# The attention output product of layer 2 as one level of Strassen in 14 block pieces

## The chip, the cores and the metric

The kernel runs on one core of a Trainium2 chip. The metric is the device time of one execution in microseconds. In the profile PE is TensorE's matmul, PEld its weight load, DVE is VectorE, ACT ScalarE, POOL GpSimd and SP SyncE.

## What is computed

Two layers on x of 512 tokens by 1024 features, all in float32. Layer 1 is a differential attention and a retention; layer 2 is a gated convolution and a sliding-window attention. The change is in layer 2:

```python
y_c = b_c * causal_depthwise_conv(c_c * v_c, conv_w)
y_c = y_c * jax.nn.silu(z_c)
y_a = jnp.einsum('bsc,cd->bsd', y_c, w_conv_out)
...
o = sliding_window_attention(q, k, v, sinks) * jax.nn.silu(z_a)
y_b = jnp.einsum('bsc,cd->bsd', o, w_attn_out)
gates = jax.nn.sigmoid(gate_logits + gate_b)
g_a, g_b = jnp.split(gates, N_BRANCHES, axis=-1)
merged = g_a * y_a + g_b * y_b
return x + jnp.einsum('bsd,de->bse', merged, w_out)
```

The product in question is `o` (512 by 1024) with `w_attn_out` (1024 by 1024).

## The kernel before

Everything runs through one stream of **weight pieces**, numbered n, of 128 by 1024 float32 (512 KB). SP loads piece n into slot n mod 4 of a ring (`w_raw`, which shares its memory with `w_lo`), once piece n - 4 is done (`wait_room`). GpSimd rounds it to `w_hi` (`round_piece`, L723), VectorE makes the rest, `w_lo = w_raw - w_hi` (`split_piece`, L1142), and TensorE multiplies. A product of two split operands is three matmuls: hi by hi, lo by hi, hi by lo (L1736 to L1738, in `products`). GpSimd and VectorE prepare piece n + 3 in their program's step n (`ROUNDED_AT`, `SPLIT_AHEAD = 3`).

Each engine's program is written out by hand as a loop over n in two halves; it waits on counting semaphores. Four pieces form a unit. Of layer 2, units 14 to 21 (pieces 56 to 87) are the convolution's inputs; beside them runs the windowed attention, step by step, up to piece 80, and its value (`gT2`) is split into `o2_hi` and `o2_lo` in the steps "OS" on VectorE (L1679, L1680). Units 22 and 23 (**pieces 88 to 95**, `U_AOUT`) are the attention output product, 24 matmuls of 512 columns each; ScalarE copies the banks to `y_b` (L968). Units 24 and 25 (96 to 103, `U_COUT`) are the convolution's output product in the same form, into `part`. From piece 104 (`GATES`) the two gate products and then (`FINAL`) the last product follow, both as one level of Strassen: seven block products A11, A12, S2, S1, S4, S3, A22 of 256 tokens, combined on VectorE.

The Strassen products need four sums of blocks of the weights. They are made in DRAM (`w_sums`): SP **copies** a block of 512 by 512 (1 MB, `copy_block`), and GpSimd's queue adds others to it by an **accumulating DMA** (`gather`, L751, 1 MB; its third and fourth step of a group wait for the landing of the ones before). Before, there are three groups of four: the two gates' and the last product's. The copies stand at pieces 20 to 27 and 48 to 51, the gathers at pieces 56, 59, 62 and so on, every third, up to 89. SP waits for the gathers of a group before it loads the first piece from it.

PSUM has eight banks: four of `proj`, two of `score`, `bank_t` and `bank_o`.

Of the kernel before, what the change touches and what calls it, by code (L numbers as in the profile page):

```python
# [30 lines left out]
P = 128  # L31
# [37 lines left out]
GROUPS = 3  # L69
# [18 lines left out]
COPY_AT = [*range(4 * U_GA, 4 * U_O0), *range(4 * U_Z0, 4 * U_Z1)]  # L88
SUM_AT = [4 * U_Z1 + 4 + 3 * i for i in range(4 * GROUPS)]
# [7 lines left out]
def slot_of(n):  # L97

    if n < GATES:
        return n % SLOTS  # L100
    return RING + n - GATES if n < GATES + EARLY else (n - GATES - EARLY) % RING
# [15 lines left out]
def unit_columns(u):  # L117
# [28 lines left out]
X_AGAIN_AT = range(4 * U_O0 + 3, 4 * U_O0 + 7)  # L146
XS_HOOKS = (7, 7, 8, 9)
# [127 lines left out]
def build(nc, a):  # L275
    with ExitStack() as ctx:
# [121 lines left out]
        m_hi = sb("m_hi", [P, KC, S], F32R, stack=later)  # L398
        logit = sb("logit", [P, 2, 2, 2, 256], stack=later)
# [35 lines left out]
        v_sum = spare[:, 0:2, 256:512]  # L435

# [10 lines left out]

        def pair_of(t, c, r):
# [35 lines left out]
        def wait_room(eng, n):  # L484
# [7 lines left out]
            elif n >= GATES:  # L492
                eng.wait_ge(piece_done, 4 * U_COUT)
# [95 lines left out]
        def wait_tile(eng, u, j):  # L589
# [3 lines left out]
            else:  # L593
                eng.wait_ge(piece_done, 4 * u + j + 1)
# [20 lines left out]

        N_PARAMS = 18
# [4 lines left out]
        def _(sp):  # L621
            def load_piece(n):
                u, q = divmod(n, 4)
                raw, landed = ring(n)[0], raw_landed[slot_of(n)]
                if n >= GATES:
# [51 lines left out]
            for n in range(SLOTS, PIECES):  # L677
# [1406 lines left out]
```

## Time and profile before

| | us |
|---|---|
| median of 3 runs | 816.91 (816.64 to 817.4) |
| the profiled execution | 816.7 |
| its span, first to last instruction | 814.7 |
| PE busy | 808.5 |
| VectorE, ScalarE, GpSimd busy | 609.4, 321.9, 182.6 |

The span lies inside the execution's time; about 2 us stand around it. In the tables below, times are microseconds from the start of the span; the attended product takes 604.6 to 648.1, the convolution's output product follows up to 691.6, then the gates up to 772.3.

### The profile page before, as it was taken

The page shows a single profiled execution, that of the slowest core. Times are in us where ns is not written, and L with a number is a line of the kernel's source. Part 1 is how long each engine was busy: PE and PEld are TensorE (multiplying, and loading weights), DVE is VectorE, ACT ScalarE, POOL GpSimd, SP SyncE. Part 2 cuts the span into 40 slices and gives each one's busy share as a digit, 9 for nine tenths or more (in the row PEclk, how much of TensorE's full clock was granted, in tenths as well). Part 3 has the DMA queues.
Part 4 walks back from the last instruction along what each step waited for, and adds up shares of the span by engine and source line. Part 5 has one row for each costly group of instructions (what it writes and reads, how often), then busy time and mean ns, then how long its engine had stood idle before and what let it go on. Part 6 is the DMA issues. An engine that isn't in the chain of part 4 may idle for free.

```text
span 814.7 us, 11429 instructions
## 1 busy us (share of the span) xinstructions
PE 808.5 (99%) x4220; PEld 687.1 (84%) x4220; DVE 609.4 (75%) x1096; ACT 321.9 (40%) x701; POOL 182.6 (22%) x189
## 2 busy tenths in 40 slices
PE   9999999999999999999999999999999999999998
PEld 7778888888888888888888888888888888999986
DVE  4998778768984476885579788978952269599998
ACT  4374465632212255334445554441000122355580
POOL 2212111111111221121324445444323224000000
PEclk9999999999999999999999999999999999999999
DMA  7332214445143222653365555566876335866562
GB/s 239 87 97 77 79 52 153 158 157 179 53 155 126 82 83 77 208 175 90 91 130 130 125 119 120 128 130 155 168 165 158 104 88 145 233 182 183 182 205 78
DMA packets 129565, 108.92 MB, mean 134 GB/s; under 512 B 4525, under 2 KB 101350, under 8 KB 129510
## 3 DMA queue, kind: packets, MB, share of 16 engines
q1 hardware_dynamic: 123142, 95.60, 38.4%
q0 software_dynamic: 6336, 12.58, 9.4%
q8 instruction: 34, 0.56, 0.3%
q14 instruction: 21, 0.17, 0.1%
q10 hardware_dynamic: 32, 0.01, 0.0%
HBM read 106.08 MB, written 27.26 MB: 164 GB/s over the span
## 4 chain that ended last, share of the span: by engine, by line
PE 92%; DVE 5%; issue 1%; ACT 1%; DVEq 0%; ACTq 0%
PE proj L1736 24%; PE proj L1738 24%; PE proj L1737 24%; PE bank_t L1750 3%; PE bank_o L1825 2%; DVE x L1447 1%; DVE w_lo L1142 1%; PE score L1738 1%; PE score L1737 1%; PE score L1736 1%; PE score L1900 1%; PE score L1899 1%; PE score L1811 1%; PE score L1810 1%; PE bank_o L1918 1%
## 5 line engine op out<-in xcount | busy, mean ns | idle before, releaser
L723 POOL TENSOR_SCALAR w_hi<-w_raw 128x1024 fp32r<-128x1024 f32 x109 | 128.8, 1182 | 436.2 <-DMA w_raw<-in_w_in_dram 310.8
L1142 DVE TENSOR_TENSOR w_lo<-w_raw,w_hi 128x1024 fp32r<-128x1024 f32 x145 | 179.9, 1244 | 60.2 <-POOL w_hi L723 59.6
L1736 PE MATMUL proj<-xt_hi,w_hi 128*128 128x512 f32 (+1 forms) x448 | 171.1, 382 | 0.0
L1738 PE MATMUL proj<-xt_hi,w_lo 128*128 128x512 f32 (+1 forms) x448 | 168.1, 375 | 0.0
L1737 PE MATMUL proj<-xt_lo,w_hi 128*128 128x512 f32 (+1 forms) x448 | 167.8, 375 | 0.0
L1738 PEld LDWEIGHTS proj<-xt_hi,w_lo 128*128 128x128 f32 x448 | 84.4, 188 | 15.5
L1737 PEld LDWEIGHTS proj<-xt_lo,w_hi 128*128 128x128 f32 x448 | 84.5, 189 | 14.2
L1736 PEld LDWEIGHTS proj<-xt_hi,w_hi 128*128 128x128 f32 x448 | 84.5, 189 | 13.9
L1736 PE MATMUL proj<-w_hi,xt_hi 128*128 128x512 f32 x152 | 61.0, 401 | 0.2 <-ACT prob L922 0.2
L1738 PE MATMUL proj<-w_hi,xt_lo 128*128 128x512 f32 x152 | 59.5, 392 | 0.0
L1737 PE MATMUL proj<-w_lo,xt_hi 128*128 128x512 f32 x152 | 59.4, 391 | 0.0
L835 ACT ACTIVATE w_hi<-w_raw 128x1024 fp32r<-128x1024 f32 x36 | 36.9, 1049 | 9.6 <-DMA w_raw<-w_sums 3.8
L1736 PE MATMUL proj<-w_hi,yc_hi 128*128 128x512 f32 x96 | 38.9, 406 | 0.0
L1738 PE MATMUL proj<-w_hi,yc_lo 128*128 128x512 f32 x96 | 37.6, 392 | 0.0
L1737 PE MATMUL proj<-w_lo,yc_hi 128*128 128x512 f32 x96 | 37.4, 390 | 0.0
L1736 PEld LDWEIGHTS proj<-w_hi,xt_hi 128*128 128x128 f32 x152 | 28.6, 188 | 6.9 <-ACT prob L922 0.7
L1038 ACT ACTIVATE prob<-prob,neg_mx 128x512 f32<-128x512 f32 x32 | 22.9, 716 | 28.3 <-DVE neg_mx L1546 28.3
L1080 ACT ACTIVATE prob<-prob,neg_m 128x128 f32<-128x128 f32 x64 | 25.0, 391 | 22.3 <-DVE sink_m L1652 22.3
L1738 PEld LDWEIGHTS proj<-w_hi,xt_lo 128*128 128x128 f32 x152 | 28.5, 188 | 6.2
L1737 PEld LDWEIGHTS proj<-w_lo,xt_hi 128*128 128x128 f32 x152 | 28.6, 188 | 6.0 <-issue 0.2
L734 POOL TENSOR_SCALAR_AFFINE_SELECT yc_hi<-pT 128x512 fp32r<-128x512 f32 x28 | 17.6, 646 | 71.4 <-ACT pT L1094 71.4
L1543 DVE CUSTOM_DVE_ANT_0 prob<-score,table 128x512 f32<-128x512 f32 x32 | 20.8, 688 | 16.1 <-PE score L1811 16.1
(420 smaller groups left out, 1774.4 us busy)
## 6 DMA issues: line engine op xcount, KB each, us to landing
w_raw<-in_w_in_dram SPq DMA_DIRECT2D x79, 512.0 KB, 3.8
w_sums<-in_w_in_dram SPq DMA_DIRECT2D x8, 1024.0 KB, 7.5
w_raw<-w_sums SPq DMA_DIRECT2D x32, 256.0 KB, 3.3
w_raw<-in_w_out_dram SPq DMA_DIRECT2D x14, 512.0 KB, 3.3
w_raw<-in_w_in_dram SPq DMA_DIRECT2D x26, 256.0 KB, 3.6
w_sums<-w_sums POOLq DMA_DIRECT2D x6, 1024.0 KB, 9.9
w_sums<-in_w_out_dram SPq DMA_DIRECT2D x4, 1024.0 KB, 6.8
w_sums<-in_w_in_dram POOLq DMA_DIRECT2D x4, 1024.0 KB, 9.9
```

Source lines behind the costliest of these rows:

```text
L723: pool.tensor_scalar(hi, raw, 1.0, 1.0, ALU.mult, ALU.mult).then_inc(hi_done, 1)
L734: pool.affine_select(out=pT_hi[:, c, :, :], in_=pT[:, 0, :, :], compare_op=op, fill=0.0, base=base, pattern=pattern, channel_multiplier=step)
L835: act.activation(hi, raw, ACT.Copy).then_inc(block_hi_done, 1)
L1038: act.activation(prob[:, m % 2, mp, :], prob[:, m % 2, mp, :], ACT.Exp, bias=neg_mx[:, m % 2, mp:mp + 1], accum_out=den[:, m % 2, mp:mp + ...
L1080: act.activation(prob2[:, m % 2, r, 0:P], prob2[:, m % 2, r, 0:P], ACT.Exp, bias=neg_m2[:, m % 4, r:r + 1], accum_out=den2[:, m % 4, r:r + 1])
L1142: dve.tensor_tensor(lo, raw, hi.bitcast(F32), ALU.subtract).then_inc(w_split, 1)
L1543: dve.tensor_tensor_reduce(prob[:, sl, mp, :], score[:, mp, :], table[:, h % 2, CENTRE - i * P:CENTRE - i * P + S], 1.0, -3e38, ALU.subtra ...
L1736: pe.matmul(out, left[0], right[0], start=first, stop=False)
L1737: pe.matmul(out, left[0], right[1], start=False, stop=False)
L1738: return pe.matmul(out, left[1], right[0], start=False, stop=last)
L1750: last = pe.transpose(dst, src, ident[:])
L1825: last = pe.matmul(bank_o[:, i * P:(i + 1) * P], wT[:, m % 2, c * P:(c + 1) * P], va[:, c, h * P:(h + 1) * P], start=(c == 0), stop=(c == 3))
```

## The change

The attended product becomes one level of Strassen. Pieces 88 to 101 (`AOUT` to `COUT`) are now 14 block pieces: for each pair of column tiles the seven products in the order A11, A12, A22, S2, S1, S4, S3, each with 2 x 4 x 3 matmuls of 256 columns. Its weights come in rows of 256 columns, from `w_attn_out_2` or from a fourth group of sums. The convolution's output product is at 102 to 109, the gates start at 110.

- GpSimd makes the four sums of blocks of the attended values in place in `gT2`, by two-input operations of 128 by 4 x 256, in its steps 84, 85, 85 and 86.
- ScalarE rounds them (steps 87 and 88), VectorE makes their low parts (steps 88, 88, 89, 90).
- In "OS" the rounding to `o2_hi` goes from VectorE to ScalarE; of the first four tiles only 256 tokens are split.
- VectorE combines the products (`combine_out`): seven operations of 512 columns for each seven products. The factor 0.5 of the copy to `y_b` moves into the gating (0.25 instead of 0.5).
- The sums of weights have 16 copies, all at pieces 12 to 27, and 16 gathers, the new group first, at pieces 53, 55, 57, 59, 62 and so on, the last five at 77, 80, 82, 84 and 86.
- The second piece of the convolution's output product waits for the last combination.

```diff
+OUT_PIECES = 7 * 2
+OUT_ORDER = [A11, A12, A22, S2, S1, S4, S3]
-COPY_AT = [*range(4 * U_GA, 4 * U_O0), *range(4 * U_Z0, 4 * U_Z1)]
-SUM_AT = [4 * U_Z1 + 4 + 3 * i for i in range(4 * GROUPS)]
+COPY_AT = range(4 * U_RQK, 4 * U_O0)
+GROUP_ORDER = [ATTENDED, 0, 1, 2]
+SUM_AT = [4 * U_Z1 + 1 + 9 * i // 4 for i in range(4 * GROUPS)]
...
+SO_SUM_AT = (AOUT - 4, AOUT - 3, AOUT - 3, AOUT - 2)
+SO_HI_AT = ((AOUT - 1, 0), (AOUT - 1, 1), (AOUT, 0), (AOUT, 1))
+SO_LOW_AT = ((AOUT, 0), (AOUT, 1), (AOUT + 1, 1), (AOUT + 2, 1))
...
+            def attended_sum(i):
+
+                x11, x12, x21, x22 = (quarter(gT2, row, col) for row in range(2) for col in range(2))
+                if i == 0:
+                    pool.wait_ge(o2_split, KC)
+                    pool.tensor_tensor(x22, x22, x21, ALU.subtract).then_inc(so_summed, 1)
+                elif i == 1:
+                    pool.wait_ge(so_summed, 1)
+                    pool.tensor_tensor(x21, x11, x21, ALU.subtract).then_inc(so_summed, 1)
...
+                if product == A12:
+                    dve.tensor_tensor(out(0, 0), u_sum, psum, ALU.add).then_inc(out_combined, 1)
+                elif product == S2:
+                    dve.tensor_tensor(w_sum, u_sum, psum, ALU.subtract).then_inc(out_combined, 1)
...
+                elif product == S3:
+                    dve.scalar_tensor_tensor(out=out(1, 1), in0=v_sum_out, scalar=-1.0, in1=psum, op0=ALU.mult, op1=ALU.subtract).then_inc(out_combined, 1)
+                    dve.tensor_tensor(w_sum, w_sum, psum, ALU.add).then_inc(out_combined, 1)
+                    dve.wait_ge(out_combined, 7 * pair + 6)
+                    dve.tensor_tensor(out(1, 0), w_sum, kept, ALU.add).then_inc(out_combined, 1)
...
+                for j in range(2):
+                    for k in range(4):
+                        last = products(out_bank(x)[:, j, :], [t[:, k, j * P:(j + 1) * P] for t in w], [t[:, k, :] for t in left], k == 0, k == 3)
+                last.then_inc(piece_done, 1)
```

GpSimd's queue around the start of the attended product. Before, from the rounding of piece 85 to that of 92 (`raw_landed3` is the landing in slot 3, and so on; the DMA rows are gathers):

```order
L723 TENSOR_SCALAR w_hi<-w_raw 128x1024 [waits piece_done,raw_landed1]
L723 TENSOR_SCALAR w_hi<-w_raw 128x1024 [waits piece_done,raw_landed2]
L751 DMA w_sums<-in_w_out_2_dram 512x512
L723 TENSOR_SCALAR w_hi<-w_raw 128x1024 [waits piece_done,raw_landed3]
L723 TENSOR_SCALAR w_hi<-w_raw 128x1024 [waits piece_done,raw_landed0]
L723 TENSOR_SCALAR w_hi<-w_raw 128x1024 [waits piece_done,raw_landed1]
L751 DMA w_sums<-w_sums 512x512 [waits w_gathered2]
L723 TENSOR_SCALAR w_hi<-w_raw 128x1024 [waits piece_done,raw_landed2]
L723 TENSOR_SCALAR w_hi<-w_raw 128x1024 [waits piece_done,raw_landed3]
L723 TENSOR_SCALAR w_hi<-w_raw 128x1024 [waits piece_done,raw_landed0]
```

And after, from the rounding of piece 85 to that of 90:

```order
L775 TENSOR_SCALAR w_hi<-w_raw 128x1024 [waits piece_done,raw_landed1]
L803 DMA w_sums<-in_w_out_2_dram 512x512
L775 TENSOR_SCALAR w_hi<-w_raw 128x1024 [waits piece_done,raw_landed2]
L775 TENSOR_SCALAR w_hi<-w_raw 128x1024 [waits piece_done,raw_landed3]
L810 TENSOR_TENSOR gT2<-gT2 128x4x256 [waits o2_split]
L803 DMA w_sums<-w_sums 512x512 [waits w_gathered2]
L775 TENSOR_SCALAR w_hi<-w_raw 128x1024 [waits piece_done,raw_landed0]
L813 TENSOR_TENSOR gT2<-gT2 128x4x256 [waits so_summed]
L816 TENSOR_TENSOR gT2<-gT2 128x4x256 [waits so_summed]
L775 TENSOR_SCALAR w_hi<-w_raw 128x1024 [waits piece_done,raw_landed1]
L819 TENSOR_TENSOR gT2<-gT2 128x4x256 [waits so_summed]
L803 DMA w_sums<-w_sums 512x512 [waits w_gathered2]
```

The four sums and two more gathers now stand ahead of the rounding of piece 90, and one step of the gathers' chain follows the other after two pieces instead of three.

VectorE at the same place, after, from the split of piece 90 (before, ten splits in a row stand there):

```order
L1232 TENSOR_TENSOR w_lo<-w_raw,w_hi 128x1024 [waits hi_done]
L1405 TENSOR_TENSOR so_lo<-gT2,so_hi 128x1024 [waits so_hi_done,so_summed]
L1232 TENSOR_TENSOR w_lo<-w_raw,w_hi 128x1024 [waits hi_done]
L1405 TENSOR_TENSOR so_lo<-gT2,so_hi 128x1024 [waits so_hi_done,so_summed]
L1232 TENSOR_TENSOR w_lo<-w_raw,w_hi 128x1024 [waits hi_done]
L1425 TENSOR_TENSOR y_b<-th2,proj 128x2x256 [waits out_first,piece_done]
L1405 TENSOR_TENSOR so_lo<-gT2,so_hi 128x1024 [waits so_hi_done,so_summed]
L1232 TENSOR_TENSOR w_lo<-w_raw,w_hi 128x1024 [waits hi_done]
L1405 TENSOR_TENSOR o2_lo<-gT2,o2_hi 128x4x256 [waits so_hi_done,so_summed]
L1232 TENSOR_TENSOR w_lo<-w_raw,w_hi 128x1024 [waits hi_done]
L1427 TENSOR_TENSOR acc<-th2,proj 128x512 [waits out_combined,piece_done]
```

The low parts of the sums and the combinations stand between the splits, each combination behind the split of the piece three further on. At the end of the product the last one, for piece 101, stands behind the split of piece 104:

```order
L1232 TENSOR_TENSOR w_lo<-w_raw,w_hi 128x1024 [waits hi_done]
L1434 SCALAR_TENSOR_TENSOR y_b<-gT2,score 128x2x256 [waits out_combined,piece_done]
L1435 TENSOR_TENSOR acc<-acc,score 128x512
L1437 TENSOR_TENSOR y_b<-acc,proj 128x2x256 [waits out_combined]
L1232 TENSOR_TENSOR w_lo<-w_raw,w_hi 128x1024 [waits hi_done]
```

Behind them on TensorE the second convolution piece waits for the last of these three.

## Rows read from the trace of the kernel before

**Rows 1.** The page: PE's busy time, and granted clock in 40 slices.

```profile
PE 808.5 (99%) x4220; PEld 687.1 (84%) x4220; DVE 609.4 (75%) x1096; ACT 321.9 (40%) x701; POOL 182.6 (22%) x189
...
PEclk9999999999999999999999999999999999999999
```

**Rows 2.** Timeline of PE (start us, us, line, op, tiles): first matmuls of stages and pieces.

```profile
604.61 0.39 PE L1736 MATMUL proj<-o_hi,w_hi 128*128 128x512 f32 x1
...
648.13 0.39 PE L1736 MATMUL proj<-yc_hi,w_hi 128*128 128x512 f32 x1
...
720.44 0.28 PE L1736 MATMUL bank_t<-sx_hi,w_hi 128*128 128x256 f32 x1
...
723.32 0.28 PE L1736 MATMUL bank_o<-sx_hi,w_hi 128*128 128x256 f32 x1
```

**Rows 3.** Busy time of each engine while the attended product runs.

```profile
core 0: us, PE busy (x) PEld busy (x) DVE busy (x) ACT busy (x) POOL busy (x), PEclk, DMA share, GB/s
604.60:648.10 43.50, 43.50 (x193) 36.04 (x192) 12.38 (x13) 4.80 (x8) 10.69 (x9) 1.00 0.58 139
```

**Rows 4.** Timeline of GpSimd: roundings of pieces 85 to 91 and two gathers.

```profile
580.20 1.05 POOL L723 TENSOR_SCALAR w_hi<-w_raw 128x1024 fp32r<-128x1024 f32 x1 [8.11 <-DMA w_raw<-in_w_in_dram]
...
583.44 1.03 POOL L751 DMA_DIRECT2D w_sums<-in_w_out_dram  x1
586.83 1.04 POOL L723 TENSOR_SCALAR w_hi<-w_raw 128x1024 fp32r<-128x1024 f32 x1 [2.36 <-DMA w_raw<-in_w_in_dram]
595.67 1.24 POOL L723 TENSOR_SCALAR w_hi<-w_raw 128x1024 fp32r<-128x1024 f32 x1 [7.79 <-DMA w_raw<-in_w_attn_out_dram]
597.65 1.97 POOL L723 TENSOR_SCALAR w_hi<-w_raw 128x1024 fp32r<-128x1024 f32 x1 [0.74 <-DMA w_raw<-in_w_attn_out_dram]
599.57 1.03 POOL L751 DMA_DIRECT2D w_sums<-w_sums  x1
...
612.88 1.05 POOL L723 TENSOR_SCALAR w_hi<-w_raw 128x1024 fp32r<-128x1024 f32 x1 [8.55 <-DMA w_raw<-in_w_attn_out_dram]
```

**Rows 5.** Timeline of VectorE: a cast slowed, a cast alone, convolution passes, splits.

```profile
582.50 1.28 DVE L1679 CAST o_hi<-gT 128x512 fp32r<-128x512 f32 x1
...
584.42 0.42 DVE L1679 CAST o_hi<-gT 128x512 fp32r<-128x512 f32 x1
...
595.25 2.20 DVE L1293 SCALAR_TENSOR_TENSOR acc<-cv,cols,acc 128x512 f32<-128x512 f32 x2
597.48 1.22 DVE L1142 TENSOR_TENSOR w_lo<-w_raw,w_hi 128x1024 fp32r<-128x1024 f32 x1
```

**Rows 6.** DMA issues (KB, us to landing) at 568.99, 572.16, 583.04, 588.48, 599.36, 599.57, 604.80.

```profile
w_sums<-in_w_out_dram POOLq DMA_DIRECT2D x1, 1024.0 KB, 9.8
...
w_raw<-in_w_in_dram SPq DMA_DIRECT2D x1, 512.0 KB, 8.0
...
w_raw<-in_w_in_dram SPq DMA_DIRECT2D x1, 512.0 KB, 3.7
...
w_raw<-in_w_attn_out_dram SPq DMA_DIRECT2D x1, 512.0 KB, 7.1
...
w_raw<-in_w_attn_out_dram SPq DMA_DIRECT2D x1, 512.0 KB, 3.8
...
w_sums<-w_sums POOLq DMA_DIRECT2D x1, 1024.0 KB, 11.9
...
w_raw<-in_w_attn_out_dram SPq DMA_DIRECT2D x1, 512.0 KB, 8.0
```

**Rows 7.** Timeline of SP's queue: when two of these loads are issued.

```profile
599.36 0.37 SPq L638 DMA_DIRECT2D w_raw<-in_w_attn_out_dram  x1
...
604.80 0.37 SPq L638 DMA_DIRECT2D w_raw<-in_w_attn_out_dram  x1
```

**Rows 8.** DMA queues in the slices 568.9:569.1 (load alone) and 588:589 (gather running).

```profile
DMA packets 132, 0.07 MB, mean 338 GB/s; under 512 B 0, under 2 KB 132, under 8 KB 132
...
q0 software_dynamic: 92, 0.19, 111.9%
```

**Rows 9.** A combination of 512 columns (ns min/median/max).

```profile
L1375 DVE TENSOR_TENSOR logit<-spare,proj x2: 686/688/689, 709.1 to 729.3; 128x512 f32<-128x512 f32 x2
```

More of the change, by code:

```diff
@@ L100, in slot_of @@
         return n % SLOTS
-    return RING + n - GATES if n < GATES + EARLY else (n - GATES - EARLY) % RING
+    if n < GATES + EARLY:
+        return RING + n - GATES
+    i = (n - GATES - EARLY) % RING
+    return i if i >= SLOTS else (i + GATES) % SLOTS
 def landings(n):
@@ L127, in unit_columns @@
             (TRA, [("w_in_2", Z2 + 512 + P * j) for j in range(4)])][u]
-    if u < U_AOUT:
+    if u < U_COUT:
         t = u - U_CONV
         return TRA, [("w_in_2", c + P * t) for c in (CV, CC, CB, CZ)]
-    t = 4 * ((u - U_AOUT) % (KC // 4))
-    return TRA, [("w_attn_out_2" if u < U_COUT else "w_conv_out_2", P * (t + j)) for j in range(4)]
+    return TRA, [("w_conv_out_2", P * (4 * (u - U_COUT) + j)) for j in range(4)]
 UNIT = [unit_columns(u) for u in range(UNITS)]
@@ L446, in left_of, with sum_of_attended, left_of_attended @@
             return [t[:, chunk:chunk + 4, token:token + 256] for t in ((hi, lo), (s_hi, s_lo))[source]]
+        def sum_of_attended(product):
+            place = {S2: 0, S1: 1, S4: 2}
+            if product == S3:
+                return [quarter(t, 1, 0) for t in (o2_hi, o2_lo)]
+            return [t[:, 4 * place[product]:4 * place[product] + 4, :] for t in (so_hi, so_lo)]
+        def left_of_attended(product):
+            source, chunk, token = LEFT[product]
+            if source:
+                return sum_of_attended(product)
+            return [t[:, chunk:chunk + 4, token:token + 256] for t in (o2_hi, o2_lo)]
         def pair_of(t, c, r):
@@ L471, in ring_parts @@
             t = ring(n)[i]
+            if AOUT <= n < COUT:
+                return [t.rearrange("p (k c) -> p k c", k=4)]
             if n >= FINAL:
@@ L593, in wait_tile @@
             else:
[L594 removed]
+                eng.wait_ge(piece_done, 4 * u + j + 1 + (OUT_PIECES if u >= U_COUT else 0))
         def wait_evacuated(eng, u, j):
@@ L614, in build, with out_bank, raw_sum @@
         gate_banks = [block_banks[b][s].rearrange("p (g s) -> p g s", g=2) for b in BANK_ORDER for s in range(2)]
+        def out_bank(x):
+            return gate_banks[(x + SLOTS) % 8]
+        def raw_sum(product):
+            return quarter(gT2, *{S1: (1, 1), S3: (1, 0), S2: (0, 0), S4: (0, 1)}[product])
         N_PARAMS = 18
@@ L775, in _ @@
                     prepare_mask()
+                for i in range(4):
+                    if SO_SUM_AT[i] == n:
+                        attended_sum(i)
                 if n in SUM_AT:
```

197 lines of the change are left out of this document (145 added, 52 removed).

## Prediction

> **What bounds the kernel now.** I read the page's busy shares first: PE is busy 808.5 of 814.7 us at a granted clock of 1.00 nearly throughout [rows 1]. A busy PE says little by itself, so I then read the starts of its matmuls in the timeline. The attended product starts at 604.61 and the convolution product behind it at 648.13 [rows 2]: 192 matmuls of 512 columns in 43.52 us, 8 pieces of 5.44 us, 0.227 us from start to start. A gate piece of 24 matmuls of 256 columns starts at 720.44 and the next at 723.32 [rows 2]: 2.88 us, 0.120 us each. Nothing waits between them, so in this stretch TensorE's columns are the time, and the other engines have room: in the attended product VectorE is busy 12.38 and GpSimd 10.69 of 43.50 us [rows 3]. What is removed from PE there is gained, if its operands come in time.
>
> **The product itself.** Removed: 8 pieces of 5.44 us, 43.52 us. Added: 14 pieces of 24 matmuls of 256 columns, at 2.88 us each, 40.32 us. **Gain 3.20 us**, all on the path. The seven eighths of Strassen (38.08 us) aren't reached, since 256 columns cost 0.120 and not half of 0.227 us.
>
> **The chain of one weight piece.** The ring has four slots in this stretch, before and after. The load of piece n is issued when piece n-4 is done, so it has three pieces of PE time to land, be rounded by GpSimd (1.05 us [rows 4]) and be split by VectorE (1.22 us [rows 5]); with the gaps between them that is 2.5 us behind the landing. Before, three pieces are 16.3 us and the landing may take 13.8 us. After, they are 8.64 us and it may take **6.1 us**. A plain landing takes 3.7 to 3.8 us [rows 6], so in the steady state there are some 2.4 us to spare.
>
> **What takes that room.** GpSimd's accumulating DMAs ("gathers", 1 MB, 9.8 to 11.9 us to landing [rows 6]). The load issued at 604.80, 5.2 us behind the gather of 599.57, lands after 8.0 us, and GpSimd can round it at 612.88 only, 1.3 us behind the gather's landing (599.57 + 11.9) [rows 4, 6, 7]. The loads of 572.16 and 588.48, issued 3.2 and 5.0 us behind theirs, take 8.0 and 7.1 us. In the slice 588:589 only the software queue moves data, at a share over 100% [rows 8]. A load issued behind a gather thus lands about 1.3 us after it, while one issued just ahead of it (599.36, against 599.57) takes 3.8 us. The Trainium skill ("DMA: Bandwidth & Descriptors", Queues, rings and completion order) says that each DMA engine takes turns between its queues packet by packet; by that only the time in which a load's data moves would double, which is 1.6 us at the 338 GB/s of a stretch with the load queue alone [rows 8]; a load beside a gather would land in 5.3 us, inside the 6.1, and the gathers would cost nothing (rival a). The rows speak against it here.
>
> **GpSimd's queue from piece 82 on** (times on the clock of before; attended pieces are 88 to 101 now). The gathers move from pieces 80, 83, 86, 89 to 80, 82, 84, 86; the four sums stand among them. The gather of 82 follows the rounding that starts at 580.20 [rows 4], so it is issued at 581.3 and lands at 591.3 to 592; the load of 87, issued at 583.0, lands behind it at 592.5 (it was rounded at 586.83 before). Then: rounding 87 to 593.6, sum, gather of 84 issued at about 596, rounding 88, two sums, rounding 89, sum, gather of 86, rounding 90. No row shows a two-input operation of GpSimd. Its one-input pass over 1024 columns takes 1.05 us [rows 4]; two inputs cost between one and three such passes, 1.05 to 3.15 us. I take 2.1, one pass for each input. The Trainium skill ("GPSIMD Engine Reference", Performance versus the Vector engine) has 4497 ns for 2048 columns, so an estimate of 2.25 us, and it speaks against the placement; by it the sums would take 0.6 us more in all. By 2.1, rounding 89 ends at 602.9, the last sum at 605.0. The gather of 86 waits for the landing of that of 84, at 606 to 608; rounding 90, whose load (599.4) is also behind the gather of 84, ends at 608.9.
>
> **The shared port.** Where a GpSimd pass and a VectorE operation on SBUF overlap, one waits: GpSimd's 1.05 us are 1.97 beside the split of 597.48, and a cast of 0.42 is 1.28 [rows 4, 5]. VectorE has about 5 us of such work between 592 and 608: three splits of 1.22 and two convolution passes of 0.75 each, one of them already held up in the 2.20 of 595.25 [rows 5]. I let half fall on GpSimd's queue, +2.5 us (ends: 0 and 5). Rounding 90 then ends near 611 and its split at 612.3; PE wants it at 604.61 + 5.76 = 610.4. **Stall 1.9 us** (0 to 6, with piece 89 at the upper end: it would be missed from 607.5).
>
> **The last gather** is issued at about 608.5. The load of 92 (607.7) is just ahead of it. That of 93 goes out when 89 is done, 610.5, lands at 608.5 + 10.5 + 1.3 = 620.3 and is ready at 622.8. PE wants it at 604.61 + 5 x 2.88 + 1.9 = 620.9. **Stall 1.9 us** (0 to 4: if the gather goes out just before 607.7, it is 92 that misses by 3 to 4).
>
> **Catching up.** For pieces 91 to 94 GpSimd's rounding (1.05), the split (1.22) and the low part of one sum (1.22) would follow each other, 3.5 us against 2.88. **1.0 us** (0 to 2.4).
>
> **The end of the product.** The second convolution piece takes the bank that holds the last A22 product, and so waits for the final three combinations. VectorE makes these behind the split of piece 104. Counted from the last product's end: load -2.7, landed 1.1, rounded 2.25, split 3.5, three combinations of 0.69 [rows 9] 5.65, then 0.2 of signalling. PE is there at 5.44. **0.4 us** (0 to 1.5).
>
> **Costed at nothing.** The casts of the attended values go from VectorE to ScalarE: neither is late there, PE has 20 us of convolution pieces above them; without this cover each cast costs 0.4 to 1.3. ScalarE's four roundings of sums lie in idle time. Combinations inside the product (0.7 us a piece) follow the splits, and banks return after 8 pieces, 23 us. Four more copies of 1 MB, all now at pieces 12 to 27, and gathers every 2.25 pieces instead of 3: loads there have three pieces of 5.4 us or more, and a landing of up to 11 us fits. If one is late in the windowed attention, where GpSimd also parts the keys, it is 0 to 1 us.
>
> **The sum.** -3.2 + 1.9 + 1.9 + 1.0 + 0.4 = +2.0 us (+2.1 with 0.1 for the attention). The profiled execution takes 816.7 us, 814.7 of it span and 2.0 around it, so 818.8; it lies 0.2 under the median of 816.9, so **819.0 us**. About 0.2%, 1.6 us, is what a measurement of this kernel can tell from no change: 815.3 to 818.5.
>
> **The rivals.**
> (a) *The queue fits.* The gathers fall between loads or slow them only a little (as by the Trainium skill's page on DMA, above), and the port costs nothing; only 0.4 us of stalls is left: 814.1 us, up to 815.3. For it: plain landings leave 2.4 us, and a load 0.2 us from a gather was untouched. Against it: loads of 2.88 us spacing can't miss a gather of 10 us, and the landings of 7.1 to 8.0. Chance 0.22.
> (b) *One stall only*, of 2 to 3.5 us, with the sums done in time: 815.3 to 817.3. Chance 0.2.
> (c) *The forecast*, stalls of 3.6 to 9 us: 817.3 to 822.5. Chance 0.48, a third of it still under 818.5.
> (d) *GpSimd's sums decide*: at 3.15 us each and the port wholly on them the rounding of 89 ends after 609 and that of 90 after 616; PE stands at 89 and 90 for 8 us, later for 2 more, and waits so long that the granted clock may fall: 822.5 to 827. It decides from about 2.5 us a sum on. Chance 0.1.
> That the change doesn't do what it says is excluded: the order shows 14 pieces of 24 matmuls of 256 columns.
>
> **How the numbers follow.** Faster by over 0.2%: (a), 0.22. Within: (b) and a third of (c), 0.36. Slower: the rest, 0.42. The range 814.2 to 823.2 leaves out (d) almost wholly and little else. The likeliest case alone is 817.3 to 822.5.
>
> **What would show it.** In the profile after: pieces of 2.88 us between stalls; PE waiting for VectorE's split (the split for GpSimd's rounding, that for a DMA) at the third and at the fifth or sixth attended piece; landings of 7 us and more for the loads of 90 and 92 or 93; GpSimd's two-input rows at 2 us or more; and a short wait at the second convolution piece. Wrong would be: a gap at the stage's start from another engine (the sums' low parts, behind splits on VectorE), a span shorter by 3 us, or stalls in the attention.

## The result

| | before | after |
|---|---|---|
| median, us | 816.95 (816.22 to 817.49) | 819.21 (818.48 to 820.84) |
| the profiled execution | 816.7 | 819.24 |
| its span | 814.7 | 817.5 |
| VectorE, GpSimd busy | 609.4, 182.6 | 636.9, 201.3 |

The changed kernel takes 1.0030 times as long, with a 95% interval of 1.0022 to 1.0038: 2.3 us by the medians, slower by a little more than the 0.2% that the measurement can tell. Of the experiments below, one execution of e4 and one of e9 took 2082 us; they are left out of the medians and the ratios.

The page of after, to be laid beside [rows 1]:

```profile
PE 808.5 (99%) x4364; PEld 693.5 (85%) x4364; DVE 636.9 (78%) x1112; ACT 325.6 (40%) x707; POOL 201.3 (25%) x203
...
PEclk9999999999999999999999999999999999999999
```

PE's busy time is what it was, although 3.2 us of columns are gone. The forty slices hide why, so the starts must be read. The timeline of PE after: the start of piece 84, of the attended product, of its third piece, of the convolution's product, and of the gates.

```profile
582.69 0.39 PE L1871 MATMUL proj<-xt_hi,w_hi 128*128 128x512 f32 x1
...
605.05 0.39 PE L1871 MATMUL proj<-o_hi,w_hi 128*128 128x256 f32 x1 [0.44 <-DVE w_lo L1232]
...
613.29 0.39 PE L1871 MATMUL proj<-o_hi,w_hi 128*128 128x256 f32 x1 [1.77 <-DVE w_lo L1232]
...
650.88 0.40 PE L1871 MATMUL proj<-yc_hi,w_hi 128*128 128x512 f32 x1
...
694.45 0.28 PE L1871 MATMUL score<-xt_hi,w_hi 128*128 128x256 f32 x1
```

and before, the first and last of these (the others are in [rows 2]):

```profile
582.85 0.39 PE L1736 MATMUL proj<-xt_hi,w_hi 128*128 128x512 f32 x1
...
691.65 0.28 PE L1736 MATMUL score<-xt_hi,w_hi 128*128 128x256 f32 x1
```

From piece 84 to the gates it was 108.80 us and is 111.76. With 14 pieces of 2.88 us and nothing waiting it would be 108.80 - 3.20 = **105.60**. So 6.2 us of stalls stand against a gain of 3.2. I call what a kernel has above 105.60 its **stalls**; this stretch holds all that moved (up to piece 84 after is 0.16 us ahead), and it lets runs be compared that differ by some tenths in the stages before.

Where the 6.2 us lie, from the starts of the pieces: 0.60 ahead of piece 88, 0.47 ahead of 89, 2.01 ahead of 90, 1.59 inside 90, 1.12 ahead of 93, 0.32 ahead of and in 94, and 0.05 at the two convolution pieces. Pieces 95 to 101 take 2.88 us each.

The 1.59 us inside piece 90 are the clock. The windows of after: PE waiting, piece 90, and what follows (columns as in [rows 3]).

```profile
611.35:613.30 1.95, 0.18 (x3) 0.01 (x1) 1.92 (x4) 0.60 (x1) 0.00 (x0) 1.00 1.08 217
614.30:617.70 3.40, 3.40 (x18) 3.40 (x18) 2.34 (x3) 0.00 (x0) 0.15 (x1) 0.50 1.07 290
617.70:620.60 2.90, 2.90 (x26) 2.90 (x26) 1.97 (x3) 0.00 (x0) 1.14 (x2) 1.00 0.61 169
```

A microsecond after PE resumes, its granted clock is 0.50 for 3.4 us, the lower of its two levels (1.2 GHz). This belongs to the traced execution and not to the median: in ten of the twelve executions the mean granted clock was 0.999 or 1.000, against 0.997 in the traced one, and their median is 819.3 us, the same. What PE waits for in those instead, no trace shows.

**What PE waited for** is VectorE's split, each time. GpSimd's timeline of after, from the first sum to the last gather:

```profile
592.68 2.39 POOL L810 TENSOR_TENSOR gT<-gT 128x1024 f32<-128x1024 f32 x1
595.01 1.03 POOL L803 DMA_DIRECT2D w_sums<-w_sums  x1
595.73 1.40 POOL L775 TENSOR_SCALAR w_hi<-w_raw 128x1024 fp32r<-128x1024 f32 x1
597.04 2.63 POOL L813 TENSOR_TENSOR gT<-gT 128x1024 f32<-128x1024 f32 x1
599.74 2.72 POOL L816 TENSOR_TENSOR gT<-gT 128x1024 f32<-128x1024 f32 x1
602.43 1.48 POOL L775 TENSOR_SCALAR w_hi<-w_raw 128x1024 fp32r<-128x1024 f32 x1
603.89 3.37 POOL L819 TENSOR_TENSOR gT<-gT 128x1024 f32<-128x1024 f32 x1
607.20 1.06 POOL L803 DMA_DIRECT2D w_sums<-w_sums  x1
```

and VectorE's beside it:

```profile
592.75 3.40 DVE L1232 TENSOR_TENSOR w_lo<-w_raw,w_hi 128x1024 fp32r<-128x1024 f32 x1 [4.31 <-POOL w_hi L775]
...
597.45 5.56 DVE L1383 SCALAR_TENSOR_TENSOR acc<-cv,cols,acc 128x512 f32<-128x512 f32 x2
603.05 1.95 DVE L1232 TENSOR_TENSOR w_lo<-w_raw,w_hi 128x1024 fp32r<-128x1024 f32 x1
604.92 0.68 DVE L1387 TENSOR_TENSOR acc<-proj,acc 128x512 f32<-128x512 f32 x1
605.63 2.71 DVE L1232 TENSOR_TENSOR w_lo<-w_raw,w_hi 128x1024 fp32r<-128x1024 f32 x1
```

A split of 1.22 us [rows 5] takes 3.40 beside the first sum, two convolution passes of 0.75 take 5.56 beside the second and third, the split of piece 89 takes 2.71 beside the fourth. That is 8.5 us more than the same five instructions undisturbed (3.40 + 5.56 + 1.95 + 2.71 = 13.62, against three times 1.22 and twice 0.75). The fifth is the split of 603.05, beside the rounding of piece 89. The instruction of 604.92, which takes one of its inputs from PSUM (`proj`), isn't held up by the fourth sum: 0.68 us. The split of 88 ends at 605.0, and PE begins 88 there; the split of 89 ends at 608.3 and PE begins 89 there. Could GpSimd's roundings be late instead, because the sums stand in its queue? Not in this trace: from 592.75 to 616 us VectorE has no idle time. The rounding of piece 89 is done at 603.9 and its split begins at 605.6; that of 90 is done by 610.4 and its split begins at 612.0, behind the convolution's steps.

The second place is the last gather. Landings after, as in [rows 6]: the gather of 607.20, the load of piece 92 issued at 608.21, that of 93 issued at 611.55.

```profile
w_sums<-w_sums POOLq DMA_DIRECT2D x1, 1024.0 KB, 10.0
w_raw<-w_sums SPq DMA_DIRECT2D x1, 512.0 KB, 9.3
...
w_raw<-in_w_attn_out_dram SPq DMA_DIRECT2D x1, 512.0 KB, 8.7
```

### The profile page after: what moved, and what is told of

Read it like the earlier page. It is cut to its first block, busy times and chain, and to the rows that moved or that the text cites. A ratio compares the mean times of both kernels' runs of the same rounds, so it can differ in the third digit from the quotient of the medians.

```text
span 817.5 us, 11794 instructions
## 1 busy us (share of the span) xinstructions
PE 808.5 (99%) x4364; PEld 693.5 (85%) x4364; DVE 636.9 (78%) x1112; ACT 325.6 (40%) x707; POOL 201.3 (25%) x203
## 4 chain that ended last, share of the span: by engine, by line
PE 88%; DVE 4%; issue 3%; POOL 2%; DMA 1%; ACT 1%; DVEq 0%; ACTq 0%; POOLq 0%
PE proj L1871 22%; PE proj L1873 22%; PE proj L1872 22%; PE bank_t L1885 3%; PE bank_o L1960 2%; DVE x L1577 1%; PE score L1871 1%; DVE w_lo L1232 1%; PE score L1873 1%; PE score L1872 1%; DMA w_raw<-in_w_in_dram 1%; PE score L2035 1%; PE score L1946 1%; PE score L1945 1%; PE score L2034 1%
## 5 line engine op out<-in xcount | busy, mean ns | idle before, releaser
L775 POOL TENSOR_SCALAR w_hi<-w_raw 128x1024 fp32r<-128x1024 f32 x115 | 133.0, 1159 | 433.4 <-DMA w_raw<-in_w_in_dram 328.7
L1232 DVE TENSOR_TENSOR w_lo<-w_raw,w_hi 128x1024 fp32r<-128x1024 f32 x151 | 194.0, 1288 | 44.9 <-POOL w_hi L775 44.3
```

The costliest lines, as they stand in the source:

```text
L775: pool.tensor_scalar(hi, raw, 1.0, 1.0, ALU.mult, ALU.mult).then_inc(hi_done, 1)
L1232: dve.tensor_tensor(lo, raw, hi.bitcast(F32), ALU.subtract).then_inc(w_split, 1)
```

## The experiments

The theory with which they began: two causes, each in its place. The sums hold VectorE up and cost 0.6 + 4.1 us ahead of and in pieces 88 to 90; the gather costs 1.1 to 1.4 us at 92 to 94. The rivals: one of them alone; the prediction's own cause (load 90, late behind a gather, decides piece 90); or gathers that cost nothing.

Ratios are to the kernel before, run on the same chip beside each group of runs (medians 816.95 to 817.58).

| kernel | stalls in the trace, us | median, us | ratio (95%) |
|---|---|---|---|
| after | 6.2 | 819.21 | 1.0030 (1.0022 to 1.0038) |
| e1: last two gathers late | 5.9 | 819.19 | 1.0020 (1.0011 to 1.0028) |
| e2: sums on VectorE | 5.2 | 818.12 | 1.0009 (1.0000 to 1.0017) |
| e3: both | 3.1 | 816.74 | 0.9986 (0.9978 to 0.9995) |
| e4: sums of 16 columns | 3.6 | 819.26 | 1.0023 (1.0012 to 1.0033) |
| e5: sums early on GpSimd | 7.9 | 822.45 | 1.0062 (1.0049 to 1.0074) |
| e6: the same, gathers late | 5.4 | 820.08 | 1.0031 (1.0019 to 1.0044) |
| e7: e6 with one gather inside | 10.8 | 825.18 | 1.0097 (1.0083 to 1.0111) |
| e8: e6 with early parts | 6.4 | 820.49 | 1.0033 (1.0021 to 1.0045) |
| e9: e3 with early sums | no trace | 815.50 | 0.9977 (0.9967 to 0.9986) |
| e12: e9 again | 1.0 | 815.49 | 0.9973 (0.9962 to 0.9984) |
| e10: e9 with early parts | 1.9 | 816.22 | 0.9981 (0.9972 to 0.9990) |
| e11: e1, sums in quarters | 6.3 | 820.03 | 1.0036 (1.0024 to 1.0048) |

Stalls less 3.2 us should be the difference to before. It agrees with the ratio to about 0.5 us in eight of the twelve traces, to 1.3 us in e1, e2 and e3 (the traced execution of e2 took 819.8 us, 1.7 over its median), and is furthest off, 1.5 us, in e4, whose single executions spread from 817.5 to 823.1 and whose traced one is the quickest of them.

### One cause, the other, both: e1, e2, e3

```diff
-SUM_AT = [4 * U_Z1 + 1 + 9 * i // 4 for i in range(4 * GROUPS)]
+SUM_AT = [4 * U_Z1 + 1 + 9 * i // 4 for i in range(4 * GROUPS - 2)] + [COUT + 1, COUT + 4]
```

> The changed kernel with its last two accumulating DMAs (the halves of the fourth sum, fired at pieces 84 and 86 of the layer) fired at pieces 103 and 106 instead, some 45 us later and still ahead of pieces 112 and 114 that read them; all four sums stay on GpSimd. After (819.2 us) carries 6.1 us over clean pieces from the attended product on: 0.6 late start and 4.1 at pieces 88 to 90, 1.1 to 1.4 at pieces 92 to 94, of which my reading gives the first part to VectorE and GpSimd holding one another up, the second to loads 92 and 93 standing 9.3 and 8.7 us behind the last accumulating DMA. Theory (both at work, each in its place): the stall at 88 to 90 stays at 3 to 4 us, pieces 92 to 94 are clean, loads 91 to 93 land in under 5 us, and the time is about 817.3 us. Rival A, the prediction's own cause (load 90 late behind the accumulating DMA decides piece 90): both stalls go, about 814.5 us. Rival B (the DMAs take turns and a gather costs nothing): 819.2 us as before.

For e2, `attended_sum` moves word for word from GpSimd's program to VectorE's (`dve.` for `pool.`):

```diff
-                for i in range(4):
-                    if SO_SUM_AT[i] == n:
-                        attended_sum(i)
...
+                    for i in range(4):
+                        if half == 1 and SO_SUM_AT[i] == n:
+                            attended_sum(i)
```

> The changed kernel with the four sums of attended values made by VectorE at the same pieces (82 to 87), the accumulating DMAs where they were. Theory (both causes): VectorE has the port to itself, its two-input instructions go back from 2.76 and 3.40 us to about 1.9, the attended product starts at 605.0 or before, pieces 88 to 90 lose under 1 us, and a stall of 2.5 to 4 us appears at 91 to 93, because loads 92 and 93 still stand behind the last accumulating DMA and nothing ahead of them has made them late: about 817.0 us. Rival A (the sums on GpSimd were all of it): 814.0 us. Rival B (the accumulating DMAs were all of it, at pieces 88 to 90 too): 819.2 us.

> Both edits at once: the sums on VectorE and the last two accumulating DMAs at pieces 103 and 106. Theory: no step of the attended product waits by more than 0.5 us, the stage takes 14 times 2.88 us = 40.3 us, and the time is that of after less its 6.1 us, 813.1 us, up to 814.0 us with what the added 10 us of work cost on VectorE: faster than the kernel before (816.95 us) by 0.4%. If either cause is still at work in a form that I have not seen (VectorE itself too late with the work of pieces 89 to 91, by the four sums that it now carries), a stall of 1 to 3 us is left at piece 89 or 90 and the time is 815 to 817 us.

In e1 the loads of pieces 90 to 95 land within 4 us of their issue, and still the attended product starts 1.0 us late and 2.55 us are lost from there to piece 92. So load 90 did not decide piece 90: **the prediction's cause for its first stall falls** (rival A, 814.5 us). The time alone doesn't tell the theory from rival B: I expected 817.3 us and measured 819.19, rival B's figure. In the trace the loads of 92 and 93 take 3.7 and 3.5 us instead of 9.3 and 8.7; that a gather costs PE time is shown further on, by e2 against e3 and by e7. But pieces 92 to 94 weren't clean either: 1.2 us are lost there, behind VectorE's own low parts and splits, and 1.2 us at the convolution's first two pieces. The timeline of VectorE in e1, and of PE:

```profile
654.79 0.68 DVE L1434 SCALAR_TENSOR_TENSOR y_b<-gT,score 128x512 f32<-128x512 f32 x1
655.39 0.68 DVE L1435 TENSOR_TENSOR acc<-acc,score 128x512 f32<-128x512 f32 x1
656.10 0.69 DVE L1437 TENSOR_TENSOR y_b<-acc,proj 128x512 f32<-128x512 f32 x1
...
656.89 0.47 PE L1871 MATMUL proj<-yc_hi,w_hi 128*128 128x512 f32 x1 [0.87 <-issue]
```

This is the wait on the last combination that the prediction priced at 0.4 us. It is 1.1 us here, where the load of piece 104 takes 4.8 us, 0.6 in e3 (4.3 us), and nothing in after (3.7 us), where the last combination ends 0.2 us before PE is there.

In e2 VectorE has no two-input instruction of GpSimd beside it, the product starts on time, and 1.05, 2.25 and 1.07 us are lost ahead of pieces 90, 91 and 92. The load of piece 91, issued at 606.19 behind the gather of 605.07, takes 9.3 us. My expectation put this stall at 91 to 93, and its size was right; the 1.05 ahead of it and the catching up make e2 1 us longer than expected. e3 missed its forecast by 3 us (813.1 to 814.0) and came out where I had put it for a cause still at work (815 to 817): 1.2 us are lost ahead of pieces 90 to 92, 1.2 behind them and 0.65 at the convolution's first two pieces.

Taken apart by the ratios, the gathers' place is worth 0.8 us (after to e1), the sums' engine 1.7 us (after to e2), both together 3.6 us (after to e3). The 0.8 isn't clear of the noise, since the intervals of after and e1 overlap. The other two are, and so is the gathers' place once the sums are on VectorE, 1.9 us (e2 to e3). Both together bring more than the sum of each, 1.1 us by the ratios (not clear of their noise) and 1.8 by the traces. I read it so: each stall **covers a part of the other**. Where PE is late already, a late load costs less.

### Only the sums' length: e4

```diff
-                x11, x12, x21, x22 = (quarter(gT2, row, col) for row in range(2) for col in range(2))
+                x11, x12, x21, x22 = (quarter(gT2, row, col)[:, :, 0:16] for row in range(2) for col in range(2))
```

> The changed kernel with the four sums on GpSimd made over 16 of each row's 256 columns only, so the most of each sum is left out; accumulating DMAs where they were. It takes GpSimd's hold on the port away and leaves the engine, the order and every wait. Theory: as with the sums on VectorE, about 817.0 us, pieces 88 to 90 clean, a stall of 2.5 to 4 us at 91 to 93. Rival A (it is not the length of the sums but their waits and their place in GpSimd's queue): 819.2 us. Rival B (the sums' length was all of it): 813.5 us.

VectorE in e4, the splits of 89 and 90, and what PE waits for in 602 to 628 (us in total, times, longest):

```profile
605.23 1.27 DVE L1232 TENSOR_TENSOR w_lo<-w_raw,w_hi 128x1024 fp32r<-128x1024 f32 x1 [4.53 <-POOL w_hi L775]
...
609.14 1.22 DVE L1232 TENSOR_TENSOR w_lo<-w_raw,w_hi 128x1024 fp32r<-128x1024 f32 x1
...
PEld score L1871 <- DVE w_lo L1232: 3.2, 2, 1.8
```

With GpSimd's sums down to 0.3 to 0.7 us each, engine, order and waits unchanged, the late start and the whole loss of pieces 88 to 90 are gone, 4.7 us; a stall of 1.8 + 1.5 us comes up ahead of 92 and 93, behind loads that take 7.8 and 7.4 us. In the trace this is the theory's picture. The median doesn't follow: 1.8 us over the traced execution, and rival A's figure. A part of the difference is the clock. The five executions with a mean granted clock of 1.000, the traced one among them, have a median of 818.0 us, which is what 3.6 us of stalls should give; the six with less took 819.1 to 823.1. Why the clock fell in those I can't say; the case for the sums as the cause rests on e2 and e3, whose medians show it.

### The sums in the idle stretch: e5, e6, e8

From 584.8 us on the attended values are split, and GpSimd stood idle to 591.7.

```diff
-SO_SUM_AT = (AOUT - 4, AOUT - 3, AOUT - 3, AOUT - 2)
+SO_SUM_AT = (AOUT - 5,) * 4
```

> The changed kernel with GpSimd's four sums all at piece 83 of the layer instead of 84 to 86, so ahead of the rounding of piece 87: the attended values are split at 584.8 us, and GpSimd stands idle from there to 591.7 us, waiting for load 87. The accumulating DMAs are where they were. Theory: the sums (about 9.5 us) fill that idle stretch and end at about 594.5, VectorE is free from then on, pieces 88 to 90 are clean, and what is left is the last accumulating DMA's 3.2 to 3.6 us at pieces 91 to 93, as in the kernel with the short sums, whose stretch from 14 us ahead of the attended product to the gates is 0.4 us longer than that of the kernel before: 0.4 to 1 us over the kernel before. Rival (a sum costs VectorE the same wherever it stands, and the stall moves to the splits of 86 and 87): no better than after, 2.4 us over the kernel before.

e6 has e1's edit besides.

> The same early sums on GpSimd, and the last two accumulating DMAs at pieces 103 and 106. Theory (the two causes found, both taken away, with GpSimd as the engine of the sums): of the 3.2 us gain about 0.2 to 1 us is lost at pieces 92 to 94 and about 0.6 us at the second convolution piece; 1.8 us under the kernel before (ratio 0.998, 815 to 816 us beside 817). Rival (GpSimd is the wrong engine wherever its sums stand; VectorE's splits and low parts of 88 to 94 are held up all the same): within 0.5 us of the kernel before, worse than with the sums on VectorE (ratio 0.9986).

Both came out beyond the rival: e5 is 4.9 us over before, where the rival had 2.4, and e6 2.5 us, where it had at most 0.5. The stage itself is clean in e6: 0.8 us of stalls in 14 pieces. But 4.6 us are lost ahead of it. VectorE in e6, beside four sums from 585.86 to 596.35:

```profile
586.41 2.39 DVE L1395 SCALAR_TENSOR_TENSOR acc<-acc,th 128x512 f32<-128x512 f32 x1
588.84 2.51 DVE L1319 CAST yc_hi<-acc 128x512 fp32r<-128x512 f32 x1
591.38 2.77 DVE L1320 TENSOR_TENSOR yc_lo<-acc,yc_hi 128x512 fp32r<-128x512 f32 x1
594.07 3.37 DVE L1232 TENSOR_TENSOR w_lo<-w_raw,w_hi 128x1024 fp32r<-128x1024 f32 x1
```

Four instructions of 0.69, 0.43, 0.69 and 1.22 us take 11 us. The sums end at 588.25, 591.05, 593.59 and 596.35, these four at 588.80, 591.35, 594.15 and 597.44. **Each gets through only when a sum has ended, one for each sum, whatever its size.** The last is the split of piece 86, for which PE then waits 3.1 us, and pays 1.5 more at the lower clock:

```profile
597.60:600.80 3.20, 3.20 (x8) 2.58 (x9) 2.43 (x2) 0.00 (x0) 3.20 (x3) 0.54 0.00 1
```

I had looked at GpSimd's idle stretch, and not at what VectorE does in it. The Trainium skill (SBUF — State Buffer, Who interferes with whom) has this as a rule: the two engines share one pair of ports under an exclusive lock. A VectorE instruction with two inputs in SBUF contends with a GpSimd instruction that reads SBUF, and one that works on both pairs of ports, as a cast can, takes the lock for its whole length if it starts first and is blocked fully if it doesn't. These rows agree, with 2.39 to 3.37 us for all four. The prediction had cited no rule and charged the lock to GpSimd's queue alone.

e8 is e6 with ScalarE's roundings and VectorE's low parts of the sums earlier:

```diff
-SO_HI_AT = ((AOUT - 1, 0), (AOUT - 1, 1), (AOUT, 0), (AOUT, 1))
-SO_LOW_AT = ((AOUT, 0), (AOUT, 1), (AOUT + 1, 1), (AOUT + 2, 1))
+SO_HI_AT = ((AOUT - 2, 1), (AOUT - 1, 0), (AOUT - 1, 1), (AOUT, 0))
+SO_LOW_AT = ((AOUT - 1, 0), (AOUT - 1, 1), (AOUT, 0), (AOUT, 1))
```

> The kernel of early sums and late accumulating DMAs, with ScalarE's roundings of the four sums half a piece to one piece earlier and VectorE's four low parts at pieces 87 and 88 (both halves each) instead of 88 to 90. In the kernel with sums on VectorE a split and a low part together took 3.1 us a piece, against PE's 2.88, so 0.24 us was lost at each of the pieces 90 to 94. Theory (VectorE's four low parts crowd the pieces 90 to 94): 0.5 to 1 us less than without this edit. Rival: they crowd pieces 88 and 89 instead, no gain or a loss of up to 1.5 us.

The rival's case, by the trace; the ratios, 1.0033 and 1.0031, don't tell the two apart. e6's 0.8 us ahead of and in piece 94 go, 1.1 us come ahead of piece 91 and 0.3 behind it.

### One gather alone inside the product: e7

```diff
-SUM_AT = [4 * U_Z1 + 1 + 9 * i // 4 for i in range(4 * GROUPS - 2)] + [COUT + 1, COUT + 4]
+SUM_AT = [4 * U_Z1 + 1 + 9 * i // 4 for i in range(4 * GROUPS - 2)] + [COUT - 7, COUT + 4]
```

> The kernel of early sums and late accumulating DMAs, with one of the two brought back into the middle of the attended product (piece 95 of the layer instead of 103), where no sum, no attended low part after the fourth and no other DMA but the loads is at work: the price of one accumulating DMA inside the product by itself. Theory (loads issued behind it land some 1 us after it, 7 to 9 us): load 98 or 99 lands after 7 us or more, one stall of 3 to 4 us at piece 98 or 99, and the time is 3 us above that of the kernel without it. Rival (each DMA engine takes turns between the queues, a load beside it lands in 5.3 us at most): no stall, and the same time as without it.

Landings in e7 of the gather (issued 636.24), of load 100 (637.02) and, in their own windows, of loads 101 (639.90) and 102 (642.78):

```profile
w_sums<-w_sums POOLq DMA_DIRECT2D x1, 1024.0 KB, 10.3
w_raw<-in_w_attn_out_dram SPq DMA_DIRECT2D x1, 512.0 KB, 9.7
...
w_raw<-w_sums SPq DMA_DIRECT2D x1, 512.0 KB, 8.3
...
w_raw<-in_w_conv_out_dram SPq DMA_DIRECT2D x1, 512.0 KB, 7.2
```

The gather lands at 646.5, the loads at 646.7, 648.2 and 650.0. They land one behind another once the gather is through, but they didn't stand still beside it. The two queues in 640 to 645 us (packets, MB, share of the 16 engines' time; q0 has the gather, q1 the loads):

```profile
q0 software_dynamic: 377, 0.77, 83.0%
q1 hardware_dynamic: 376, 0.39, 28.2%
```

They take turns, packet for packet. But a packet of the gather carries 2 KB and holds an engine three times as long as a load's of 1 KB, so the load gets 0.39 MB in 5 us, 78 GB/s instead of the 338 of [rows 8]. At other times a load didn't move at all: in after, 600 to 602 us, the gather has 202 packets and the load of piece 90 none, and before, 589 to 591 us, it is 183 against none. Why it is the one or the other, no run shows. PE's wait here:

```profile
649.15 0.39 PE L1871 MATMUL score<-so_hi,w_hi 128*128 128x256 f32 x1 [3.52 <-DVE w_lo L1232]
```

One gather among pieces of 2.88 us costs 3.7 us of waiting and 1.6 of the lower clock in piece 100, **5.1 us by the medians of e7 and e6**; I had expected 3, at piece 98 or 99, and no clock. It is the dearest single thing found here, and after pays little of it only because its gather comes when PE is late anyway. By the Trainium skill's rule of turns packet by packet (DMA: Bandwidth & Descriptors, Queues, rings and completion order), which stood behind rival (a) of the prediction, the queues alternate; the 377 and 376 packets of e7 agree with it, the 202 and none of after don't. What the prediction drew from the rule, that a load beside a gather loses only the time in which its data move and lands in 5.3 us, falls in e7 in either case. Two loads got by: in e2 one issued 0.56 us behind a gather landed after 6.3 us, 3 us ahead of the gather, and in e4 one issued 0.07 us behind landed after 4.2.

### Is the port held by the instruction: e11

On e1, each sum is made in four instructions of 128 by 256.

```diff
+                for c in range(4):
+                    last = pool.tensor_tensor(*(x[:, c:c + 1, :] for x in (out, left, right)), op)
+                last.then_inc(so_summed, 1)
```

> The changed kernel with the last two accumulating DMAs late (ratio 1.002), and each of GpSimd's four sums made as four instructions of 256 columns instead of one of 1024: the same engine, place and work. In the traces so far a VectorE instruction issued beside a two-input instruction of GpSimd ended with it, after 2.4 to 3.4 us, whatever its own size (0.43 to 1.22 us). Theory (the port is held for the length of one instruction): VectorE gets in between the quarters, none of its instructions takes more than its own time and 0.7 us, the late start of 0.6 us and most of the 2.3 us at pieces 88 to 91 go, 2 to 2.5 us less: 816.8 us beside 817.5. Rival (the two engines share the port by turns all the time, so that only the total of the work counts): the same time as with whole sums, 819.1 us, or more by the fixed cost of 12 further instructions.

GpSimd in e11:

```profile
593.87 4.00 POOL L815 TENSOR_TENSOR gT<-gT 128x256 f32<-128x256 f32 x4
...
599.30 7.13 POOL L815 TENSOR_TENSOR gT<-gT 128x256 f32<-128x256 f32 x8
606.40 1.05 POOL L775 TENSOR_SCALAR w_hi<-w_raw 128x1024 fp32r<-128x1024 f32 x1
```

The last six of these eight, from a window that begins inside them:

```profile
602.11 4.32 POOL L815 TENSOR_TENSOR gT<-gT 128x256 f32<-128x256 f32 x6
```

VectorE:

```profile
593.94 1.75 DVE L1229 TENSOR_TENSOR w_lo<-w_raw,w_hi 128x1024 fp32r<-128x1024 f32 x1 [4.99 <-POOL w_hi L775]
...
607.55 1.68 DVE L1229 TENSOR_TENSOR w_lo<-w_raw,w_hi 128x1024 fp32r<-128x1024 f32 x1 [5.41 <-POOL w_hi L775]
```

The mechanism holds: a split beside the quarters takes 1.75 and 1.68 instead of 3.40 and 2.71, and the product starts on time. The forecast of the time was wrong by over 3 us: 1.0036, and e1 had 1.0020. Now GpSimd is behind. The first two of the eight quarters take 2.8 us beside VectorE's work. The other six take 4.32 us, 0.72 each, with VectorE idle from 602.1 on, so not all of their length is the port: a quarter of 2.39 is 0.60. The rounding of piece 89 stands behind them and starts at 606.40 (603.74 in e1, although piece 84 starts 0.4 us later there), and VectorE stands idle for 5.4 us waiting for it. PE loses 1.44 and 3.27 us ahead of 89 and 90, and 1.58 at the lower clock. So there are two bounds, the port and GpSimd's queue; easing the one showed the other.

### The sums in VectorE's idle stretch: e9, e12, e10

e9 is e3 with e5's edit: all four sums in one row ahead of the split of piece 87, where VectorE waited for load 87.

> The kernel with the sums on VectorE and the last two accumulating DMAs late (ratio 0.9986), with all four sums at piece 83, in one row ahead of the split of piece 87, where VectorE stood idle for 4.3 us (588.45 to 592.75 in after) waiting for load 87. Theory (what was left there, 0.8 us at piece 89 and 0.24 at 90 and 91, was VectorE behind with its own sums): four sums of 1.23 us make the split of 87 late by 0.7 us at most, which PE doesn't see; pieces 88 to 91 are clean, and 0.8 us at pieces 92 to 94 and 0.6 us at the second convolution piece are left of the 3.07: 815.7 us beside 817.5 (ratio 0.998). Rival (the early sums cost there what they cost on GpSimd, since the place is the trouble): a stall of over 3 us at pieces 86 to 88, slower than the kernel before.

> The kernel of e9_vector_early once more, unchanged, for its trace: sums on VectorE in one row ahead of the split of piece 87, last two accumulating DMAs late. Theory: ratio 0.9975 to 0.998 again; in the trace four sums of 1.2 us from about 588.5 us, the first alone to be held up being the fourth (beside a rounding of GpSimd), pieces 88 to 91 clean, and what is left over 2.88 us a piece, 1.0 to 1.5 us in all, at pieces 92 to 94 and in front of the second convolution piece. Rival: the gain over the kernel of both edits (0.9986) is another's, and pieces 89 to 91 carry the same 1.2 us as there.

The trace is that of e12, the same kernel once more. VectorE's sums:

```profile
589.75 1.22 DVE L1385 TENSOR_TENSOR gT<-gT 128x1024 f32<-128x1024 f32 x1
591.00 1.23 DVE L1388 TENSOR_TENSOR gT<-gT 128x1024 f32<-128x1024 f32 x1
592.26 1.23 DVE L1391 TENSOR_TENSOR gT<-gT 128x1024 f32<-128x1024 f32 x1
593.52 2.00 DVE L1394 TENSOR_TENSOR gT<-gT 128x1024 f32<-128x1024 f32 x1
```

and all that PE waits for from 590 to 660 us:

```profile
PEld score L1871 <- DVE w_lo L1213: 0.5, 1, 0.5
PEld proj L1871 <- issue: 0.3, 1, 0.3
PEld bank_t L1871 <- DVE w_lo L1213: 0.2, 1, 0.2
```

The product is 41.1 us, 43.5 before. Stalls are 1.0 us: 0.8 ahead of 93 and 94, and 0.25 around the second convolution piece. It is 1.8 to 2.2 us quicker than the kernel before, and about 4.5 us quicker than after (the theory had 815.7 us): **the version that beats both.**

> The same, with ScalarE's roundings of the sums half a piece to a piece earlier and VectorE's four low parts half a piece earlier each (from the second half of piece 87 on; before, from piece 88 on). Theory (the 0.8 us at pieces 92 to 94 are VectorE with a split of 2.05, a low part of 1.21 and combinations in one 2.88 us piece): 0.3 to 0.8 us less than without this edit, 815.2 us. Rival: the crowd moves to piece 89 or 90, as with the sums on GpSimd, and the time is the same or up to 1 us more.

Here `SO_HI_AT` is as in e8 and `SO_LOW_AT` is `((AOUT - 1, 1), (AOUT, 0), (AOUT, 1), (AOUT + 1, 1))`. Again the crowd moves: 1.1 us ahead of piece 91. By the traces the old places are better by 0.9 us (stalls of 1.0 and 1.9); the intervals of the ratios overlap.

## Why the prediction was right, point by point

The time was right to 0.2 us (819.0 against 819.21) and so was the sign that it held likeliest, but part of its working wasn't: the sum of stalls was 5.3 and is 6.0 with the stretch before, and the terms are other ones.

- **The gain, 3.20 us**: right. Pieces 95 to 101 take 2.88 us each.
- **Costed at nothing, the start of the stage**: 0.6 us late, since the split of 88 stood behind held-up instructions. The prediction had named this sign among those that would show it wrong.
- **Stall at piece 90, 1.9 us**: 2.5 us, ahead of 89 and 90, and 1.6 of lower clock behind them. The step that failed is the cause. The load of 90 landed at 605.4, well inside its time; e1 shows the stall without any late load. What I missed is under "the shared port": I let half of 5 us fall on GpSimd's queue and none on VectorE, whose five instructions lost 8.5 us. The half on GpSimd came out, 2.3 us over its four sums and the roundings of 88 and 89; the pass itself was nearly right, 2.39 us where I took 2.1.
- **The clock**: I had it fall only in rival (d), after 8 us of waiting. It fell after 2.0. Its 1.6 us in piece 90 are a term of the trace, not of the median: the executions in which it didn't fall take as long, perhaps because the load of 93 would have kept PE waiting anyway.
- **The last gather, 1.9 us at piece 93**: right in place and mechanism, 1.1 us in size, because PE was 4.7 us late by then and not 1.9. Where PE was in time it was 3.2 (e4) to 3.7 us (e7).
- **Catching up, 1.0 us**: 0.3 in after; the mechanism shows in e3, where 0.2 to 0.8 us are lost ahead of each of the pieces 91 to 94.
- **End of the product, 0.4 us**: 0.05 in after, 0.06 to 1.2 in the others. Right in mechanism; its last step, 3.5 and three times 0.69, gives 5.57 and not 5.65, which is 0.1 us less.
- **The attention with four more copies and closer gathers, 0.1 us**: nothing; piece 84 starts 0.16 us earlier.
- **What takes the room**: the slice 588:589 of [rows 8] comes too early to show a load of 588.48 standing still, since that of 599.36 has no packet before 600.0 either, with nothing beside it. The reading held even so (589 to 591 us, above). For the loads of e7 it didn't.
- **Rival (a)** fell with e7, **(d)** in its main part: no sum took 2.5 us of its own work, but its side remark on the clock came true.

That the total came so near is partly luck: with the clock, the sums cost 4.7 us where I had 1.9, and the last gather, the catching up, the end and the attention cost 1.3 us where I had 3.4.

## What to carry to other kernels

Work given to GpSimd is not free because GpSimd is idle: look at what VectorE has to do in those microseconds, and reckon up to one whole GpSimd instruction of delay for each cast or instruction with two inputs in SBUF that VectorE has beside one with two inputs. Before shortening the pieces of a weight stream, move every bulk DMA out of the shortened stage; a landing that hid behind three long pieces stands bare behind three short ones. And since stalls in a row cover each other, take them away together before judging what each is worth.

## What the runs showed of the hardware that I had not expected

- A cast of 0.43 us on VectorE took 2.51 beside a two-input instruction of GpSimd. That instruction took 2.39 us where it came first and 2.5 to 3.4 behind one of VectorE's; the same sum on VectorE takes 1.23 us.
- Cutting GpSimd's instruction in four has its own price: a quarter took 0.72 us with VectorE idle, where a quarter of 2.39 is 0.60, and 1.4 beside VectorE's work (e11).
- With waits of 2.0 us (after), 3.0 to 3.1 (e5, e6, e8), 3.3 (e11) and 3.7 (e7) PE's granted clock fell to the lower level for some 3 us, between 0.5 us before PE resumed (e6) and 1.3 us behind (e8), and 1.5 to 1.7 us were lost each time. With waits of 1.05, 2.25 and 1.07 us close to each other (e2) it stayed at 1.00 in the traced execution, and in most executions of after it didn't fall either.
- Loads issued 0.8 to 3 us behind an accumulating DMA landed 0.2 to 0.9 us after it (after, e2, e4, e7), and in e7 the next ones 1.5 and 1.8 us apart, so at 350 and 290 GB/s, near the 338 of a load alone [rows 8]. Beside it the two queues moved packet for packet, 2 KB against 1 KB, or the load not at all.
- An instruction of VectorE with one input in PSUM took its own 0.68 us beside a sum of GpSimd (after, 604.92), where a split took 2.71.
